# The rotary half swap on TensorE in place of SBUF-to-SBUF DMAs

## The reference

```python
def apply_rope(t, cos, sin):
    t1, t2 = jnp.split(t.astype(jnp.float32), 2, axis=-1)
    c = cos[None, :, None, :]
    s = sin[None, :, None, :]
    return jnp.concatenate([t1 * c - t2 * s, t2 * c + t1 * s], axis=-1).astype(t.dtype)

def hybrid_mixer(h, w_in, ...):
    u = h @ w_in
    (z, xs, bs, cs, dt_raw, fq, fk, fv, ff, mq, mk, mv, dq, dk, dv, iq, ik, iw) = jnp.split(u, ...)
    y_ssm = mamba2_branch(z, xs, bs, cs, dt_raw, ...)
    y_fox = fox_branch(fq, fk, fv, ff, ...)
    y_moba = moba_branch(apply_rope(mq), apply_rope(mk), mv)
    y_dsa = dsa_branch(apply_rope(dq), apply_rope(dk), dv, apply_rope(iq), apply_rope(ik), iw)
    ...
```

## Time and profile before

| | |
|---|---|
| time, median of 3 runs | 2331.8 us (2330.97 to 2332.16) |
| the profiled execution | 2331.8 us, its span 2330.0 us |
| granted TensorE clock, mean | 0.998 |
| TensorE busy | 2280.7 us, 98% |
| VectorE busy | 1442.2 us, 62% |
| ScalarE busy | 1119.5 us, 48% |
| DMA engines, share of the span | 51.1% |

### The profile page before, as it was taken

The page is one execution under the profiler, slowest core; times in us unless marked ns, Lnnn a source line. Parts: engine busy times, 40 slices in busy tenths (PEclk is TensorE's granted clock), DMA queues, the critical chain, the costliest instruction groups (busy, mean ns, idle before and its releaser), DMA issues.

```text
span 2330.0 us, 37794 instructions
## 1 busy us (share of the span) xinstructions
PE 2280.7 (98%) x16500; PEld 2141.9 (92%) x16500; DVE 1442.2 (62%) x1558; ACT 1119.5 (48%) x1417; POOL 64.4 (3%) x58
## 2 busy tenths in 40 slices
PE   7999999999999999999999999999999999999998
PEld 6999998998899999899789998999888999899986
DVE  4767557445667746645677767455557775745554
ACT  4545544434564464534455444444445544444443
POOL 0000000000000000000000000000000000000000
PEclk9999999999999999999999999999999999999999
DMA  7544455555664446556544434446555443444653
GB/s 240 157 145 141 145 190 181 181 191 181 177 183 127 137 128 208 180 181 217 179 128 126 137 109 163 145 160 185 207 174 155 128 128 110 165 142 163 192 197 108
DMA packets 300665, 378.14 MB, mean 162 GB/s; under 512 B 26383, under 2 KB 260821, under 8 KB 300501
## 3 DMA queue, kind: packets, MB, share of 16 engines
q1 hardware_dynamic: 300500, 375.73, 51.1%
HBM read 369.67 MB, written 1.05 MB: 159 GB/s over the span
## 4 chain that ended last, share of the span: by engine, by line
PE 94%; DVE 3%; ACT 2%; DMA 0%; issue 0%; POOL 0%; POOLq 0%; SPq 0%; DVEq 0%; ACTq 0%
PE ps L582 26%; PE ps L2124 21%; PE ps L2680 7%; PE ps L2135 5%; PE ps L923 5%; PE ps L834 4%; PE ps L2194 3%; PE ps L2183 2%; PE ps L631 2%; PE ps L595 2%; PE ps L869 2%; PE ps L850 1%; PE ps L762 1%; PE ps L728 1%; PE ps L2403 1%; PE ps L2418 1%
## 5 line engine op out<-in xcount | busy, mean ns | idle before, releaser
L582 PE MATMUL ps<-a_nhi,a_wlo 128*128 128x256 f32 x1664 | 477.7, 287 | 0.0
L582 PE MATMUL ps<-a_nhi,a_whi 128*128 128x256 f32 x1664 | 471.2, 283 | 0.0
L582 PE MATMUL ps<-a_nlo,a_whi 128*128 128x256 f32 x1664 | 471.2, 283 | 0.0
L1204 DVE TENSOR_TENSOR a_wlo<-a_ring,a_whi 128x2048 fp32r<-128x2048 f32 x174 | 395.9, 2287 | 115.5 <-ACT a_whi L949 114.8
L3010 DVE TENSOR_TENSOR b_wlo<-b_ring,b_whi 128x2048 fp32r<-128x2048 f32 (+1 forms) x168 | 379.7, 2262 | 129.4 <-ACT b_whi L2705 129.2
L949 ACT CAST a_whi<-a_ring 128x2048 fp32r<-128x2048 f32 x174 | 331.4, 1905 | 191.5 <-PE ps L582 59.7
L2705 ACT CAST b_whi<-b_ring 128x2048 fp32r<-128x2048 f32 (+1 forms) x168 | 316.6, 1884 | 142.1 <-PE ps L2680 79.1
L2124 PE MATMUL ps<-b_nhi,b_wlo 128*128 128x256 f32 x1232 | 357.3, 290 | 2.5 <-ACT b_gates L2760 1.6
L2124 PE MATMUL ps<-b_nhi,b_whi 128*128 128x256 f32 x1232 | 348.8, 283 | 0.0
L2124 PE MATMUL ps<-b_nlo,b_whi 128*128 128x256 f32 x1232 | 348.8, 283 | 0.0
L582 PEld LDWEIGHTS ps<-a_nhi,a_wlo 128*128 128x128 f32 x1664 | 319.6, 192 | 3.0 <-issue 2.3
(11 more groups left out here) (581 smaller groups left out, 4537.8 us busy)
## 6 DMA issues: line engine op xcount, KB each, us to landing
a_ring<-in_w_in SPq DMA_DIRECT2D x50, 1024.0 KB, 5.4
b_ring<-in_w_in SPq DMA_DIRECT2D x50, 1024.0 KB, 5.9
a_ring<-in_w_ffn_in SPq DMA_DIRECT2D x44, 1024.0 KB, 5.3
a_ring<-in_w_gate SPq DMA_DIRECT2D x32, 1024.0 KB, 5.3
b_ring<-in_w_up SPq DMA_DIRECT2D x32, 1024.0 KB, 5.5
b_ring<-in_w_down SPq DMA_DIRECT2D x32, 1024.0 KB, 5.1
a_ring<-in_w_ffn_out SPq DMA_DIRECT2D x22, 1024.0 KB, 5.0
a_ring<-in_w_branch SPq DMA_DIRECT2D x16, 1024.0 KB, 5.2
```

Source lines behind the costliest of these rows:

```text
L582: mm = T.matmul(out, w[:, k, c:c + P], x_[:, k, :], start=k == 0 and n == 0, stop=k == KD - 1 and n == 2)
L1204: nc.vector.tensor_tensor(part(wlo, h), part(ring, h), part(whi, h).bitcast(F32), ALU.subtract).then_inc(lo_ok, 1)
```

## The change

The half swap moves from the DMAs to TensorE. A 128x128 matrix of 0, 1 and -1 (`rot`, in the first block's constants) has for each output feature the partner and its sign. `turn` multiplies it with the tile in one plain fp32 matmul of 512 or 256 columns, halfway through a fill, ahead of what else `mid` issues. Its output takes a unit of `order` and so one of the two banks; VectorE frees it by the first step of `rope`, which reads the bank. `TURNS` says at which slot each is issued; VectorE does the rope in the iteration of the same number. The swap buffers, SP's waits and 40 transfers a layer go away.

```diff
-C1_COS, C1_SIN, N_CONST1 = 0, 256, 640
+C1_COS, C1_SIN, C1_ROT, N_CONST1 = 0, 256, 512, 640
@@ shape_constants_1
-    c[:, C1_SIN:C1_SIN + SEQ] = np.sin(ang) * np.where(r % 64 < 32, -1.0, 1.0)[:, None]
+    c[:, C1_SIN:C1_SIN + SEQ] = np.sin(ang)
+    for m in range(P):
+        k = m + 32 if m % 64 < 32 else m - 32
+        c[k, C1_ROT + m] = -1.0 if m % 64 < 32 else 1.0
@@
-ROPE = [("iqk", 0, 2, 9, 14, 12), ("iqk", 2, 1, 4, 14, 12), ("mq", 0, 2, 14, 19, 17), ("mq", 2, 2, 15, 20, 18),
-        ("mk", 0, 2, 17, 22, 20), ("mk", 2, 2, 18, 23, 21), ("dk", 0, 2, 16, 25, 23), ("dk", 2, 2, 21, 26, 24),
-        ("dq", 0, 2, 22, 28, 26), ("dq", 2, 2, 23, 29, 27)]
+TURNS = {10: [("iqk", 0, 2)], 11: [("iqk", 2, 1)], 15: [("mq", 0, 2)], 16: [("mq", 2, 2)], 19: [("mk", 0, 2)],
+         20: [("mk", 2, 2)], 22: [("dk", 0, 2)], 23: [("dk", 2, 2)], 24: [("dq", 0, 2)], 25: [("dq", 2, 2)]}
@@ order
     for i in range(4, N_IN1 + N_GATE1):
         order += [("in", i, n) for n in range(len(IN1[i][2]))] if i < N_IN1 else [("gate", i - N_IN1)]
+        order += [("turn", name, at_) for name, at_, _ in TURNS.get(i, [])]
     unit = {key: u for u, key in enumerate(order)}
-    freed = [(free_a, n + 1) for n in range(len(order))]
-    filled = {key: n + 1 for n, key in enumerate(order)}
+    freed, n_freed = [], {free_a.name: 0, free_v.name: 0}
+    for key in order:
+        by = free_v if key[0] == "turn" else free_a
+        n_freed[by.name] += 1
+        freed.append((by, n_freed[by.name]))
+    turns = [key for key in order if key[0] == "turn"]
+    filled = {key: n + 1 for n, key in enumerate(key for key in order if key[0] != "turn")}
@@ sync
-            for r, (name, at_, n, src, issued, _) in enumerate(ROPE):
-                if issued == h:
-                    t, to = dst[name][:, at_:at_ + n, :], (swap0, swap1)[r % 2][:, 0:n, :]
-                    sp_.wait_ge(*freed[unit["in", src, 0]])
-                    if r >= 2:
-                        sp_.wait_ge(free_v, r - 1)
-                    for q in range(4):
-                        sp_.dma_start(to[32 * q:32 * q + 32], t[32 * (q ^ 1):32 * (q ^ 1) + 32]
-                                      ).then_inc(swap_in[r % 2], 16)
@@ tensor
+        def turn(name, at_, n):
+            src = H_FEW if (name, at_) == ("iqk", 2) else \
+                [j for j in range(4, N_IN1) if any(p[3:] == (name, at_) for p in IN1[j][2])][0]
+            b = bank(("turn", name, at_))
+            pe.wait_ge(*freed[unit["in", src, 0]])
+            pe.wait_for(con1_in, 32)
+            T.matmul(b[:, 0:n * SEQ], rot, dst[name][:, at_:at_ + n, :], start=True, stop=True
+                     ).then_inc(turn_ps, 1)
@@ mid
+            for name, at_, n in TURNS.get(i, []):
+                turn(name, at_, n)
             if i == 12:
                 state_scores()
@@ rope
-            dve.wait_ge(swap_in[r % 2], 64 * (r // 2 + 1))
+            dve.wait_ge(turn_ps, r + 1)
...
-            V.tensor_tensor(rt[:, 0:n, :], (swap0, swap1)[r % 2][:, 0:n, :],
+            V.tensor_tensor(rt[:, 0:n, :], ps[:, u % 2, 0:n * SEQ].rearrange("p (a b) -> p a b", a=n),
                             sin.unsqueeze(1).broadcast_to([P, n, SEQ]), ALU.mult).then_inc(free_v, 1)
@@ vector, iteration i
-            for r in range(len(ROPE)):
-                if ROPE[r][5] == i:
-                    rope(r)
+            for name, at_, n in TURNS.get(i, []):
+                rope(name, at_, n)
```

More of the change, by code:

```diff
@@ L141 @@
 GAINED_1 = {
-    "gpost_in": 64, "landed0": 464, "landed1": 528, "landed2": 464, "par_in": 64, "small_in": 64, "sgw_in": 320,
-    "w_small": 320, "tr_ps": 8, "full": 42, "half_used": 34, "par_ps": 1, "few_ps": 1, "cum_ps": 1, "cb_ps": 1,
-    "xs_ps": 1, "dec_ps": 8, "ix_ps": 2, "y_ps": 1, "qk_ps": 12, "yt_ps": 4, "pt_ps": 6, "o_ps": 6, "pr_ps": 16,
+    "gpost_in": 64, "landed0": 464, "landed1": 528, "landed2": 464, "par_in": 64, "small_in": 64, "tr_ps": 8,
+    "full": 42, "half_used": 34, "par_ps": 1, "few_ps": 1, "turn_ps": 10, "cum_ps": 1, "cb_ps": 1, "xs_ps": 1,
+    "dec_ps": 8, "ix_ps": 2, "y_ps": 1, "qk_ps": 12, "yt_ps": 4, "pt_ps": 6, "o_ps": 6, "pr_ps": 16,
     "out_used": 3, "mix_ps": 2, "dn_ps": 2, "in_ms": 4, "hi_ok": 87, "nhi_ok": 8, "free_a": 42, "spe": 3,
@@ L147 @@
     "sig_ok": 2, "yh_ok": 4, "mh_ok": 4, "ssq_ok": 6, "ms_ok": 6, "fg_free": 11, "hh_ok": 11, "xn_ok": 8,
-    "lo_ok": 87, "nlo_ok": 8, "pad_ok": 2, "par_ok": 1, "spv": 2, "lcat_ok": 1, "cum_ok": 2, "free_v": 10,
-    "rope_ok": 10, "xs_ok": 1, "sc_ok": 2, "msq_ok": 1, "mx_ok": 12, "yt_ok": 1, "pn_ok": 12, "pt_v": 6,
+    "lo_ok": 87, "nlo_ok": 8, "pad_ok": 2, "par_ok": 1, "spv": 2, "lcat_ok": 1, "free_v": 10, "rope_ok": 10,
+    "cum_ok": 2, "xs_ok": 1, "sc_ok": 2, "msq_ok": 1, "mx_ok": 12, "yt_ok": 1, "pn_ok": 12, "pt_v": 6,
     "isc_ok": 1, "pen_ok": 2, "yl_ok": 4, "pr_free": 16, "mg_ok": 14, "ml_ok": 4, "x_ok": 4, "fu_free": 11,
@@ L250, in first_block @@
     cos, sin = con1[:, C1_COS:C1_COS + SEQ], con1[:, C1_SIN:C1_SIN + SEQ]
+    rot = con1[:, C1_ROT:C1_ROT + P]
     ring = at("ring", [P, SLOTS, PART])
@@ L270, in first_block @@
     hhi, hlo = (at(n, [P, SPLITS, 2 * SEQ], F32R, offset=base + i * 6144) for i, n in enumerate(("hhi", "hlo")))
-    swap0 = at("swap0", [P, 2, SEQ], offset=base + 14336)
     base = place[0]
@@ L318, in first_block @@
     eps = at("eps", [P, 1])
-    swap1 = at("swap1", [P, 2, SEQ])
     assert place[0] <= 229344, place[0]
@@ L328, in first_block @@
     con1_in = sem("con1_in")
-    swap_in = [sem("sgw_in"), sem("w_small")]
     par_in, small_in, gpost_in = sem("par_in"), sem("small_in"), sem("gpost_in")
@@ L332, in first_block @@
     hi_ok, lo_ok = sem("hi_ok"), sem("lo_ok")
-    full, free_a, free_v = (sem(n) for n in ("full", "free_a", "free_v"))
+    full, turn_ps, free_a, free_v = (sem(n) for n in ("full", "turn_ps", "free_a", "free_v"))
     par_ps, par_ok = sem("par_ps"), sem("par_ok")
@@ L1325, in softplus_3, with rope @@
             ins.then_inc(lcat_ok, 1)
-        def rope(r):
-            name, at_, n = ROPE[r][:3]
+        def rope(name, at_, n):
+            u = unit["turn", name, at_]
             t = dst[name][:, at_:at_ + n, :]
-            dve.wait_ge(swap_in[r % 2], 64 * (r // 2 + 1))
+            r = turns.index(("turn", name, at_))
+            dve.wait_ge(turn_ps, r + 1)
             if r:
```

## The result

| | before | after |
|---|---|---|
| time, median | 2331.98 us (2330.97 to 2332.6) | 2362.75 us (2361.33 to 2363.77) |
| span of the profiled execution | 2330.0 us | 2360.9 us |
| granted TensorE clock | 0.998 | 0.997 |

The ratio is 1.0132, with a 95% interval of 1.0114 to 1.0149. The changed kernel takes 30.8 us more; 32.1 us were forecast.

A forecast was written before the change was run, and what follows sets the result against it. TensorE, never idle in the projection stretch, was taken as the bound: 2331.8 us plus turns 16.3 and waits 15.8 gave 2363.9 us, 1.4% slower, with an 8-in-10 range of 2352 to 2375 us.

The forecast's parts named there:

- TensorE is the bound here, and what is put on it is put on the end: First block's projection stretch: TensorE busy 140.00 of 140.00 us, so each microsecond added there lengthens the run.
- The swaps are worth 0: Projection stretch: removing the DMA swaps gains 0, since slot 14's late weights still leave 5.5 us of slack.
- Ten turns a layer, 8.2 us: TensorE, projection stretch: nine turns at 0.86 us and one at 0.43, 16.3 us in two layers.
- A wait at the next fill, 1.0 us: After a turn, the next fill takes the preceding fill's bank and waits for ScalarE's eviction: 0.93 + 0.08 us where uncovered.
- `y_turn`, 1.5 us: Behind fill 19: rope stands ahead of `y_normed` on VectorE, so `y_turn` starts late, costing 1.4 + 0.08 us a layer.
- The other ropes stay covered: VectorE's other ropes moved forward delay nothing; slacks 1.4 us at `p_turn(0)`, about 2.0 in iteration 22, 2.6 in 25.
- 14 waits of ScalarE's evictions: Sign in the changed profile: about 14 new TensorE waits for ScalarE's evictions, 0.8 us each.
- the turns alone: Rival: the bank waits don't show because there is more cover, only the turns cost; 2348 us, chance 0.06.
- the cheap pass: Rival: a turn costs one cheap pass on TensorE, 2.2 us a layer; 2352 us, chance 0.03.
- VectorE behind: Rival: ropes ahead of `normalise` in iterations 19, 22, 25 delay TensorE; 2380 us, or 2372 with half; chance 0.11.
- the clock: Rival: each of 16 waits makes TensorE's granted clock fall, 42 us more; 2406 us, chance 0.04.
- not slower: Rival: swaps hold weights back at slot 14, removal outweighs the turns; 2326 us, chance 0.04, half within 0.2%.

The follow-up runs named there:

- turns alone: Kernel before, swaps kept, with ten added plain fp32 matmuls a layer on constants, written into the idle fill bank: 2347.10 us, ratio 1.0067.
- the waits alone: Kernel before, swaps kept and no turn, with empty gaps in the order of units so that fills land in the preceding fill's bank: 2345.56 us, ratio 1.0061.
- the last experiment: Changed kernel with turns borrowing the next fill's bank, y_normed ahead of the rope, and each turn one reduced-format product on a rounded copy: 2338.00 us, ratio 1.0027.
- the second profile of the changed kernel: The changed kernel run again, unchanged, as the measure for the repairs beside it: 2363.61 us, ratio 1.0136.

## Why the prediction was right, step by step

- *TensorE is the bound here, and what is put on it is put on the end.* Shown: with turns alone the whole price reaches the time.
- *The swaps are worth 0.* Shown: 0.9999 without them, the wait at slot 14 gone and unused.
- *Ten turns a layer, 8.2 us.* Measured 8.1 by the distance. The prediction's estimate from the Trainium skill of 0.52 us for a large turn, from "TensorE: Matmul & The Clock Gate", Back-to-back issue gap, is not borne out: the row shows 0.86. The Trainium skill's four passes, from "FP8 and Floating Point Precision" (TensorE Precision Notes), would fit it, at 0.215 us each. The trace shows two records for a turn, so that there are four passes is not shown.
- *A wait at the next fill, 1.0 us.* Shown three ways: as the new entries of the changed kernel, made alone without a turn, and taken away with the turns kept. The place of each came out: 0.78 us of idle time behind fills 11 and 15, 0.15 behind 10, none behind 16 and 24. Fill 15 had been put at 1.1 us for a ScalarE that is busy; it lost 1.0 like the others. Where 7.5 us a layer was expected of the waits alone, 7.3 was measured.
- *`y_turn`, 1.5 us.* The wait of 1.20 us is there, and the whole loss is 1.4 us. It falls with one swap of two lines on VectorE, for 1.3 us a layer.
- *The other ropes stay covered.* They did, with no new wait for `a_probs` or `a_wlo`. How thin this was shows the last experiment, where `p_turn` does wait.
- *14 waits of ScalarE's evictions.* 13 show in the entries of the first block. The fourteenth, behind fill 10 in layer 1, has no entry, yet TensorE restarts there at 668.87, 0.14 us after the eviction's end at 668.73, as at the others.
- *Sum.* 16.05 us a layer was worked out, 15.8 measured, so this part is no luck. Two layers give 31.6 us, and the span grew by 30.9. Two things outside the projection stretch make the rest, and the prediction had neither. TensorE came to its first 256 column product of the stream at 41.0 us and not at 42.4; over the ten profiles this lies anywhere from 41.0 to 42.4, and the second profile of the changed kernel has 42.0. And between the two blocks 0.7 us more is lost. There the granted clock is at its low level, 1.2 GHz, for 6.8 us in both profiles, but from 1162.7 us before and from 1194.9 after, which is 3.0 and 5.0 us behind the last product ahead of TensorE's wait. In the changed kernel less of the low stretch falls into the wait. 31.6 - 1.4 + 0.7 = 30.9. That these two took no more than 0.7 us off together is luck.

The rivals fell: the turns alone by the waits, the cheap pass by 0.86 us, VectorE behind by the absence of waits for `normalise`, the clock by 0.997 with 15 short idles at 1.00, and not slower by all of it. The price of the clock rival was read too low: the low stretch of the earlier trace rows lasts from 1162.7 to 1169.5, 6.8 us and not 5.5, so 16 falls would have cost some 54 us, by the same half, and not 42. For the clock the Trainium skill's section on psum-queue depth-cycling spoke, in "TensorE: Matmul & The Clock Gate"; here 13 idles of 0.15 to 0.84 us from a cycled bank, and two of 1.20 us for `y_normed`, brought no fall.

## What to carry to other kernels

When work is moved onto an engine, ask two things apart: what it costs there, and which buffer it takes from the work around it. Here each was about half of the loss, and the diff names only the first: the second follows from one line that puts a unit into `order`, which puts the unit's two neighbours in one bank. And where the bound engine never waits for a transfer, look for no gain from taking it away: here 80 transfers were worth nothing.

## What the runs showed of the hardware

A plain fp32 matmul of 512 columns costs the stream 0.86 us, one of 256 columns 0.43, and one 512 column product of the reduced format 0.23. Easy to miss in a profile: a wait for a bank costs 0.93 + 0.08 us even when the evicting engine stands idle for it, of which the eviction is only 0.60. And 40 small transfers a layer between SBUF and SBUF, with SP's waits for them, raised the DMA share of the first stretch from 0.44 to 0.51 and held ScalarE 3.05 us for one slot of weights, yet cost the kernel nothing that can be measured (0.9999).
